# Recurrence: single loads between GpSimd's operations in place of bursts

## The reference

```
w: decay, a: in-context rate, kk: normalised key, k_t: key scaled by a and k_a
S <- S * w  -  (S kk) (kk * a)^T  +  v k_t^T        # forward over the tokens, and backward
y  = S r                                             # both directions are added
y  = groupnorm(y) * ln_g + ln_b + sum(r * k_t * r_k) * v, then times the gate g
```

## Time and profile before

| what | value |
| --- | --- |
| median of three runs | 5036.0 us |
| the profiled execution | 5046.98 us, span 5045.7 us |
| TensorE matmuls busy | 4561.1 us, 90% |
| VectorE, ScalarE busy | 1396.9 us (28%), 1160.2 us (23%) |
| GpSimd busy | 501.3 us, 10% |
| mean granted TensorE clock | 0.959 |
| the recurrence | about 3478 to 4400 us of the span; a pair takes some 113 us |

### The profile page before, as it was taken

The page is one execution under the profiler, slowest core; times in us unless marked ns, Lnnn a source line. Parts: engine busy times, 40 slices in busy tenths (PEclk is TensorE's granted clock), DMA queues, the critical chain, the costliest instruction groups (busy, mean ns, idle before and its releaser), DMA issues. The chain is left out here.

```text
span 5045.7 us, 97660 instructions
## 1 busy us (share of the span) xinstructions
PE 4561.1 (90%) x42830; PEld 2480.6 (49%) x42830; DVE 1396.9 (28%) x3428; ACT 1160.2 (23%) x2445; POOL 501.3 (10%) x570
## 2 busy tenths in 40 slices
PE   8999999999998899786999997996888888779998
PEld 6775444444444344554444433444666666544343
DVE  1032110010001221433122225023555655432222
ACT  2032111002101222423222112023333333221111
POOL 0000000000002002002000000125332232010000
PEclk9999999999999899997999998998999999879999
DMA  3143111221222113431878874234000010029998
GB/s 132 67 152 126 67 67 60 78 82 67 81 83 62 51 50 100 136 97 59 294 283 292 296 285 156 88 118 145 23 29 29 29 35 10 13 89 408 408 407 342
DMA packets 256434, 680.55 MB, mean 135 GB/s; under 512 B 23600, under 2 KB 66464, under 8 KB 255760
## 3 DMA queue, kind: packets, MB, share of 16 engines
q1 hardware_dynamic: 234048, 608.24, 33.0%
q0 software_dynamic: 21968, 66.07, 4.4%
HBM read 644.76 MB, written 26.74 MB: 133 GB/s over the span
## 5 line engine op out<-in xcount | busy, mean ns | idle before, releaser
L2235 PE MATMUL bank<-ring,arena 128*128 128x512 f32 x2592 | 1127.8, 595 | 16.8 <-DVE arena L1967 11.0
L2235 PEld LDWEIGHTS bank<-ring,arena 128*128 128x128 f32 x2592 | 559.6, 217 | 561.6 <-issue 476.6
L2604 PE MATMUL bank<-ring,arena 128*64 128x512 f32 x2048 | 470.3, 598 | 11.1 <-DMA ring<-in_moe_w 7.0
L2235 PE MATMUL bank<-arena,ring 128*128 128x512 f32 x1024 | 443.0, 595 | 1.6 <-ACT arena L1208 0.9
L1912 DVE TENSOR_TENSOR arena<-arena,bank 128x512 f32<-128x512 f32 x300 | 187.1, 682 | 651.4 <-PE bank L2577 582.5
L2235 PEld LDWEIGHTS bank<-arena,ring 128*128 128x128 f32 x1024 | 195.1, 191 | 247.1 <-issue 244.8
L2604 PEld LDWEIGHTS bank<-ring,arena 128*64 128x64 f32 x2048 | 139.6, 136 | 313.4 <-issue 308.2
L2630 PE MATMUL bank<-ring,arena 128*64 128x512 f32 x1024 | 233.7, 604 | 2.3 <-ACT arena L1426 1.6
L2406 PE MATMUL bank<-ring,arena 128*128 128x512 f32 x512 | 219.9, 592 | 0.0
L1419 ACT ACTIVATE arena<-bank 64x512 f32<-64x512 f32 x64 | 37.6, 588 | 663.7 <-PE bank L2604 663.7
L2866 PE MATMUL bank<-arena 64*64 64x128 f32 x3840 | 160.0, 273 | 2.4 <-issue 2.2
(11 more groups left out here) (405 smaller groups left out, 5772.6 us busy)
## 6 DMA issues: line engine op xcount, KB each, us to landing
ring<-in_moe_w SPq DMA_DIRECT2D x768, 512.0 KB, 7.6
ring<-in_w_in SPq DMA_DIRECT2D x21, 2048.0 KB, 7.8
ring<-in_ada_w SPq DMA_DIRECT2D x12, 2048.0 KB, 8.0
ring<-in_ada_w SPq DMA_DIRECT2D x24, 1024.0 KB, 5.5
ring<-in_w_up SPq DMA_DIRECT2D x8, 2048.0 KB, 9.0
ring<-in_w_down SPq DMA_DIRECT2D x8, 2048.0 KB, 7.8
ring<-in_na_w_qkv SPq DMA_DIRECT2D x6, 2048.0 KB, 7.8
ring<-in_w_in SPq DMA_DIRECT2D x8, 1024.0 KB, 6.4
```

What stands on the lines that cost most here:

```text
L2235: ins = mm(ps[:, 0:ncol], lhs(k), rhs(k), start=(k == 0 and first), stop=(k == nk - 1))
L2604: ins = mm(ps, x_chosen[:, b, k, 0:CAP_L], w[x][:, n * W:(n + 1) * W], start=(k == 0), stop=(k == KD - 1))
```

## The change

Both bursts are taken apart. `load_pair` is split into `load_one` and `load_rows`. The row load of the early set stays behind `weigh_bonus(p)`, but the six early loads of pair p+2 are issued within `factors(p+1)`, three in each z: behind the first, the second and the fourth operation. The wait for the first product T moves behind the second operation. Of the late set, v and the rows stay where they are, and g is issued within the next `weigh_bonus`, between its fifth and sixth operation. The loads of pairs 0 and 1, ahead of the loop, stay as they are.

```diff
--- before.py
+++ after.py
@@ -1091,10 +1091,15 @@
             pool.dma_start(dst if len(dst.shape) == 2 else dst.rearrange("p a b -> p (a b)") if len(dst.shape) == 3 else
                            dst.rearrange("p a b c -> p (a b c)"), a[name]).then_inc(sem("rw_const_landed"), 16)
 
+        def load_one(p, q, signal):
+            pool.dma_start(RW_IN[q][p % 2], spill[q][p]).then_inc(sem(f"{signal}_{p % 2}"), 16)
+
         def load_pair(p, names, rows, signal):
             for q in names:
-                pool.dma_start(RW_IN[q][p % 2], spill[q][p]
-                               ).then_inc(sem(f"{signal}_{p % 2}"), 16)
+                load_one(p, q, signal)
+            load_rows(p, rows, signal)
+
+        def load_rows(p, rows, signal):
             pool.dma_start(rw_rows[:, p % 2, rows], a["rw_rows"][rows, p * P:(p + 1) * P].partition_broadcast(P)
                            ).then_inc(sem(f"{signal}_{p % 2}"), 16)
 
@@ -1123,22 +1128,32 @@
         def across(row, nt):
             return row.unsqueeze(1).to_broadcast([P, nt, P])
 
-        def factors(p):
+        def factors(p, loads=()):
 
             I, k_a = {q: v[p % 2] for q, v in RW_IN.items()}, rw_rows[:, p % 2, 1, :]
             early_landed(pool, p)
             pool.wait_ge(sem("rw_keys_ready"), p + 1)
             if p >= 2:
                 full(pool, "rw_y", p - 2, RW_STEPS - 1, 1)
+            loads = list(loads)
+
+            def load_next():
+                if loads:
+                    load_one(p + 1, loads.pop(0), "rw_early_landed")
+
             for z in range(2):
                 az, B, T = I[f"a{z}"], bh[p % 2][z], th[p % 2][z]
-                link(G.tensor_tensor(T, az, across(k_a, NT), ALU.mult))
+                t_ready = G.tensor_tensor(T, az, across(k_a, NT), ALU.mult)
+                load_next()
                 G.tensor_tensor(B, kk, az, ALU.mult)
+                load_next()
+                link(t_ready)
                 link(G.tensor_tensor(T, T, across(k_a, NT), ALU.subtract))
                 link(G.tensor_tensor(T, T, I["k"], ALU.mult))
+                load_next()
                 G.tensor_tensor(T, T, I["k"], ALU.add).then_inc(sem("rw_factors"), 1)
 
-        def weigh_bonus(p):
+        def weigh_bonus(p, loads=()):
 
             I, k_a, r_k = {q: v[p % 2] for q, v in RW_IN.items()}, rw_rows[:, p % 2, 1, :], rw_rows[:, p % 2, 2, :]
             w = yd[0]
@@ -1152,6 +1167,8 @@
             for _ in range(2):
                 link(G.tensor_tensor(w, w, across(k_a, LT), ALU.subtract))
             link(G.tensor_tensor(w, w, I["k"][:, 0:LT], ALU.mult))
+            for q in loads:
+                load_one(p, q, "rw_late_landed")
             for _ in range(2):
                 link(G.tensor_tensor(w, w, I["k"][:, 0:LT], ALU.add))
             link(G.tensor_tensor(w, w, I["r"], ALU.mult))
@@ -1159,17 +1176,18 @@
 
         factors(0)
         for p in range(RW_PAIRS):
-            weigh_bonus(p)
+            weigh_bonus(p, LATE[1:] if p >= 2 else ())
             if p + 2 < RW_PAIRS:
                 pool.wait_ge(sem("rw_bonus_weighed"), p + 1)
                 pool.wait_ge(sem("rw_scaled"), rw_scaled(p, "R", 1))
                 full(pool, "rw_side", p, "sum_ex", 1)
-                load_early(p + 2)
+                load_rows(p + 2, slice(0, 3), "rw_early_landed")
             if p + 1 < RW_PAIRS:
-                factors(p + 1)
+                factors(p + 1, EARLY if p + 2 < RW_PAIRS else ())
             if 1 <= p < RW_PAIRS - 1:
                 pool.wait_ge(sem("rw_read_out"), p)
-                load_late(p + 1)
+                load_one(p + 1, LATE[0], "rw_late_landed")
+                load_rows(p + 1, slice(3, 5), "rw_late_landed")
         taken(pool, "rw_ot", RW_PAIRS - 1)
         pool.dma_start(rw_gate, mod_dram[1, 0, 2 * D:3 * D].partition_broadcast(P)).then_inc(sem("rw_gate_landed"), 16)
         experts(1)
```

## The result

The changed kernel takes 5059.5 us in the median of seven runs (5045.7 to 5075.6), against 5036.0 (5029.7 to 5039.7) for the kernel before. The ratio is 1.0043, with a 95% interval of 1.0029 to 1.0058. I had forecast 5024 with a range of 5009 to 5040, so the direction was wrong too. The profiled run of the changed kernel is the longest of the seven, 5075.6 us with a span of 5074.3.

What follows compares the result with a forecast made beforehand. TensorE, busy for 90% of the span, was taken as the bound, stalled by late instruction pages. The terms -16.4 + 4.2 - 1.6 + 1.8 = -12.0 us took the median from 5036.0 to 5024, range 5009 to 5040.

Steps and rivals of the forecast that it cites:

- The page stall, term (a): Behind weigh_bonus, the early-load burst delays an instruction page and stops TensorE; moving those loads wins 16.4 us.
- Late pages in factors: In factors, instruction pages sometimes find a moved load ahead of them; costs 0.7 us per pair, +4.2 us.
- The g load: In weigh_bonus, half of the 0.54 us that issuing g there could win per pair; -1.6 us in all.
- The moved wait: In factors, the wait for the first product T goes behind the B product; no effect on the time.
- The shared port: In factors, loads between GpSimd operations lengthen their holds against VectorE; +0.3 us per pair, +1.8 us in all.
- The slower rival: Longer factors run holds the L2052 pair and two L2021; 6.5 us per pair, 39 in all, 5061 us; chance 0.10.

Runs made afterwards that it cites:

- all_waits: The changed kernel with a wait behind each of the ten operations of factors and each load behind such a wait; 5026.0 us, 0.9992 of the kernel before.
- g_back: The changed kernel with the g load back in the late burst behind factors, early loads still between the operations; 5060.8 us, 1.0052 of the kernel before.
- wait_only: The kernel before with only the wait for the first product T moved behind the B product, all loads in their bursts; 5036.7 us, ratio 0.9998.
- wait_back: The changed kernel with the wait for T directly behind T again, loads still between the operations; 5054.3 us, 1.0041 of the kernel before.

## Why the prediction was wrong

- *The page stall, term (a), -16.4 us: right.* The four stretches fell by 3.0 us each where 3.6 was taken, and leaving the loads out wins 15 us (10 to 20). That the burst's length makes the stall holds too: pacing with the same traffic removes it. That it is a page that comes late remains an inference.
- *Late pages in factors, +4.2 us: too much.* The gap that stands in factors has DVE L2108 as its releaser, not "issue". The "issue" waits in the four factors stretches are 1.2 us in all in the kernel before, 0.4 in the changed one, and 2.1 in all_waits, which issues the same loads at almost the same pace. all_waits loses 2 us per pair there in all, and waits on held instructions account for most of it: in the pair at 3983 TensorE waits 2.0 us for L2108 and 1.4 for L2070, where before it waits 0.8 for L2090.
- *The g load, -1.6 us: open.* It is below what can be told: g_back and the changed kernel can't be told apart.
- *The moved wait, nothing: right by itself* (wait_only). With loads in the chain it decides where the hold ends: one of 6.9 us, or two of 2.6 and 3.9 (wait_back).
- *The shared port, +0.3 us per pair with bounds of -0.6 and +2.1: this is the step that failed.* It measured 6.4 us per pair in the factors stretch, clock included. I had read rightly from the earlier trace rows that an operation queued behind a load holds the port during the load's issue. I then took as the upper bound one load and one operation, 0.54 + 1.54. The hold ends at the next wait that GpSimd comes to, and the changed code has no such wait from the last load of z = 0 to the subtraction of z = 1: two load issues and four operations, 7.5 us (4018.39 to 4025.88). I looked for the price at the scan step L2052 near the end of the run. It fell on L2090, a short addition in its middle that TensorE waits for directly, and that the trace of before shows stretched to no more than 0.77 us, once 1.27 in the first pair.
- *The slower rival* put the loss at the port and came to 5061 us, near the 5059.5 measured. The nearness is luck: it reached 6.5 us per pair from four waits of at most one load and one operation each, and the runs show one hold over three times as long as that. It had other victims too (L2052 and L2021; L2021 was one in a single factors run, in g_back), and a chance of only 0.10. It was put low because "the new end reaches only the first pair of operations". That counted which operations come within reach of a longer run, and not how long GpSimd goes without a wait.

The Trainium skill ("SBUF — State Buffer", section "Who interferes with whom") has a VectorE instruction with two SBUF inputs contend with a GpSimd instruction that reads SBUF. By it, as the prediction read it, a load between two operations would be free time for VectorE. For runs with no load in them the trace agrees (wait_only, 0.54 and 0.77 us). Behind a load it does not (2.12 us in all_waits), and the measurement decides.

**What stays open.** Why a load makes the difference. The runs show where the hold ends, at the next wait that holds GpSimd, in three patterns of waits. They show that it can begin within the issue of a load (all_waits, g_back) or in an operation behind one (the changed kernel at 4019.31, wait_back). They don't show what in GpSimd's queue passes the port on. That the late pages are TensorE's is still inferred, from "issue" gaps that go when the burst is paced or left out, and why a page comes through one burst and not another isn't known.

## What to carry to other kernels

Loads that GpSimd issues don't belong among GpSimd operations that share SBUF with a busy VectorE. Put them where GpSimd has nothing behind them, or put a wait behind every operation, and then count one load and one operation as the hold. A burst of 2.4 MB of loads stopped TensorE here for 2.6 to 4.75 us; pacing it by its own landings, in idle time of the issuing engine, brought most of that back. When GpSimd has a load in a chain of operations, count the time to its next wait that holds, and look for the short VectorE instructions with two SBUF inputs that something waits for directly.

## What the runs showed of the hardware that I had not expected

- A VectorE addition with both inputs in SBUF was held for 6.9 us by GpSimd over two load issues and the operations around them; four GpSimd operations in a row without loads held it for 0.77 us, 1.44 in the first pair.
- The hold can begin during the issue of a load, with no GpSimd operation running: an addition started at 3989.84, inside a load issue of 3989.51 to 3990.09, waited for the operation behind it (all_waits).
- A 6 us stop of TensorE is followed by a stretch at the lower clock: 0.50 granted in the 3.8 us behind it and 0.99 in the next 4.0, and 0.82 to 0.88 over the 28 us around it, where the kernel before shows 1.00 at the same place.
- The traffic alone does little harm: 62 to 66 GB/s paced cost 0.5 us in the stretch (33.4 against 32.9 us with no early loads), 46 to 58 GB/s with a burst cost 3.4 (36.3).
